# A two-block transformer kernel on one core: a mixer's first token tile transposed among the MLP's last row products, the second token tile transposed later at norm edges, and opening chunk pairs multiplied 512 columns wide outside the second block's mixers

## The chip, the cores and the metric

The kernel runs on 1 core of one Trainium2 chip. The metric is the device time of one execution in microseconds (us), and the median of several runs is compared. TensorE (PE) multiplies, VectorE (DVE) and ScalarE (ACT) do the elementwise work, GpSimd (POOL) computes small factors and starts some loads, SyncE (SP) starts the loads of weights.

## The reference, cut to what matters

A sequence of 256 tokens of width 1024 goes through two blocks, all in float32.

```python
def first_block(x, ...):                       # 2 layers
    for l in range(DEPTH):
        x = layer_norm(ALPHA * x + 0.5 * swiglu(x, wg0, wu0, wd0), ...)   # D_FF = 2816
        x = layer_norm(ALPHA * x + token_mix(x, w_in, w_out, ...), ...)   # three attention forms side by side
        x = layer_norm(ALPHA * x + 0.5 * swiglu(x, wg1, wu1, wd1), ...)
def second_block(x, ...):                      # 4 layers; mixers: delta rule, mLSTM, differential attention, delta rule
    for i in range(DEPTH_2):
        x = x + rms_norm(mixer_i(rms_norm(x, g0)), g1)
        x = x + rms_norm(square(relu(rms_norm(x, g2) @ w1)) @ w2, g3)     # D_FF_2 = 4096
```

## The kernel before

**Chunks.** All weights pass through the core once, as 365 chunks of 1 MB. A column chunk holds 256 output columns of a projection, with all 1024 input rows as 8 steps k of 128. A row chunk holds 256 input rows of a down projection with all 1024 output columns. Every chunk goes through SP's load into a slot of `raw` (5 slots), ACT's `split_high` (a rounded copy into one of 4 slots of `w_hi`, L461), DVE's `split_low` (the rest into `w_lo`, which lies over `raw`, L468), and three matmuls (hi by hi, hi by lo, lo by hi, `product`, L482 to L484). `load_chunk` waits until the chunk five places earlier has been used, `split_high` until the one four places earlier has. The semaphore `weights_used` counts used chunks. SP, ACT and DVE each go through the chunks in one fixed order, and each engine's queue is in order: a wait holds up all that is behind it.

**Stages.** First block: ffn(0,0), mix 0, ffn(0,1), ffn(1,0), mix 1, ffn(1,1). Second block, for i from 0 to 3: mixer i (delta rule, mLSTM, differential attention, delta rule) and mlp i. n0 is a stage's first chunk, and n0+1 and so on are the next. The MLP's order is hidden 0, hidden 1, hidden 2, rows 0, hidden 3, rows 1, hidden 4, rows 2, and so on to three row chunks at the end. So n0+3 is rows 0, n0+4 hidden 3, n0+5 rows 1 and n0+6 hidden 4.

**Between stages (an edge).** The sums y of a stage lie in PSUM banks 0 to 3, two banks for each tile of 128 tokens. `last_rows` (L624) finishes them bank by bank with the last row chunks. DVE and ACT then make the next input of tile 0 and of tile 1. PE transposes it in halves of four 128x128 blocks (`turn_bank`, L890 on: L897, or L895 as a matmul with a diagonal of token factors, which takes two passes), ACT copies the bank to aT_hi (L904), and DVE writes the rest to aT_lo (L910). A norm edge (in and after the first block) has x as input (written at L965). For the edges into ffn and mix, PE does a part of tile 0's transposes inside `last_rows` (`turn_first`). In the second block the input H is x times a gain; its token factor comes through POOL and a diagonal (L1743), but the third mixer takes H without the factor (`factor_behind`).

**The opening (`open_stage`, L566).** A stage's first two chunks n0 and n0+1 are column chunks that are multiplied in pieces, so that tile 0 can run while tile 1 is still being made: n0 steps 0 to 3, n0+1 steps 0 to 3, n0 steps 4 to 7, then `turn_tile(1)` (PE waits there for tile 1's input), n0+1 steps 4 to 7, and then tile 1 of both chunks. Before the MLPs after the delta rule ("early" edges) n0 has all of tile 0 first. All matmuls of the opening move 256 columns. n0 counts as used three quarters through the opening, n0+1 at its end; chunk n0 accumulates in bank 0, n0+1 in bank 1.

**The MLP's first hidden chunks.** Hidden 0 and 1 come out with tokens on the partitions, so PE transposes them (`turn_hidden`, L695): both in the middle of hidden 2, into banks 2 and 6. ACT copies (L700) and DVE writes the rest (L704). From hidden 2 on, the product stands the other way round (`wide_product`, L512 and L514) and needs no transposes. Hidden 3 writes banks 6 and 7.

Of the kernel before, what the change touches and what calls it, by code (L numbers as in the profile page):

```python
# [8 lines left out]
ALU = mybir.AluOpType  # L9
# [243 lines left out]
def two_block_model(nc, w, out):  # L253
# [311 lines left out]

    def open_stage(pe, n, edge):  # L566
# [8 lines left out]
        if n == 0:  # L575
            for q in range(4):
# [3 lines left out]
                tokens_steps(pe, 0, 0, 0, FIRST[0][q])  # L580
            turn_tile(pe, edge, 1)
            wait_part(pe, first_lo, lo_ready, 1, 0)
            tokens_part(pe, 1, 1, 0, 0)
            for half in range(2):
                turned_set(2 + half)
                last = tokens_part(pe, 0, 0, 1, half)
            last.then_inc(weights_used, 1)
            wait_part(pe, first_lo, lo_ready, 1, 1)
            tokens_part(pe, 1, 1, 0, 1)
            for half in range(2):  # L590
                last = tokens_part(pe, 1, 1, 1, half)
# [19 lines left out]
        tokens_part(pe, n, 0, 0, 1)  # L611
        turn_tile(pe, edge, 1)
        tokens_part(pe, n + 1, 1, 0, 1)
# [10 lines left out]
    def last_rows(pe, chunks, turn, turn_next=None):  # L624
# [3 lines left out]
        for b in range(4):  # L628
            t, c = b // 2, slice(b % 2 * 512, b % 2 * 512 + 512)
            for q, (n, l_hi, l_lo, wait) in enumerate(chunks):  # L630
# [5 lines left out]
                for r in range(2):  # L636
                    if b == 3 and turn_next is not None and (q, r) in turns:
# [68 lines left out]
    def hidden_made(dve, hid, s, gate, up, gates):  # L706
# [3 lines left out]
        nc.vector.tensor_tensor(hidden_buffer(s), gate, up, ALU.mult).then_inc(hid_made, 1)  # L710
# [35 lines left out]
    def ffn_scalar(act, l, j):  # L746
# [3 lines left out]
        for u, (kind, s) in enumerate(FFN_ORDER):  # L750
# [2774 lines left out]
```

## Time and profile before

| what | value |
| --- | --- |
| median of 3 runs | 2362.12 us (2359.69 to 2362.32) |
| the profiled execution's own time | 2360.35 us |
| its span, first to last instruction | 2358.6 us |
| granted TensorE clock, mean over the span | 0.999 of full speed |
| PE busy | 2325.4 us, 16820 matmuls |
| DVE, ACT, POOL busy | 1567.7, 1157.1 and 159.1 us |
| moved by DMA | 405.14 MB, mean 172 GB/s |

A row of the timeline gives the start, the time taken, the engine, the line, output<-inputs, shapes and count; in brackets stands the idle time just before and who ended it. The ends of matmuls are modelled, so that the time of one matmul in steady flow is read from the distance between two starts.

### The profile page before, as it was taken

Reading aid. Unit: us, or ns where it says so; the run is one execution under the profiler, and the core shown is the slowest. Engines: PE = TensorE matmul, PEld = TensorE weight load, DVE = VectorE, ACT = ScalarE, POOL = GpSimd, SP = SyncE. Lnnn points to the kernel's source line nnn. Section 1 sums busy time; section 2 is a strip of 40 time slices with the busy share of each in tenths; the row PEclk is TensorE's granted clock in tenths of the full one; section 3 lists DMA queues with packets and bytes.
Section 4 is the critical chain, followed back from the end, with each engine's and each line's share of the span. In section 5 each row is a group of like instructions: output and inputs, shape, how many; then the busy total and the mean of one; then the engine's idle time right before and its main releaser. Section 6 shows DMA issues by size and latency. Waiting matters only on the chain. (4 is left out here: it accounts for less than half of the span.)

```text
span 2358.6 us, 39266 instructions
## 1 busy us (share of the span) xinstructions
PE 2325.4 (99%) x16820; PEld 2062.5 (87%) x16820; DVE 1567.7 (66%) x2133; ACT 1157.1 (49%) x1573; POOL 159.1 (7%) x177
## 2 busy tenths in 40 slices
PE   9999999999999999999999999999999999999998
PEld 8889888888889888899888899888898888998887
DVE  5566775666576865768666657766677656867665
ACT  5444744435435644466554445534465334665432
POOL 0100000020000100002210000100001001012000
PEclk9999999999999999999999999999999999999999
DMA  7766355666655466453265644556445565433662
GB/s 247 244 214 137 108 186 189 214 187 214 209 148 150 127 210 208 145 168 109 73 214 189 205 154 143 181 194 213 154 142 177 187 206 156 139 110 108 205 210 94
DMA packets 320829, 405.14 MB, mean 172 GB/s; under 512 B 48720, under 2 KB 281264, under 8 KB 320656
## 3 DMA queue, kind: packets, MB, share of 16 engines
q1 hardware_dynamic: 314992, 383.50, 51.6%
q0 software_dynamic: 5664, 19.13, 2.6%
q8 instruction: 133, 2.18, 0.4%
q14 instruction: 40, 0.33, 0.0%
HBM read 401.55 MB, written 1.05 MB: 171 GB/s over the span
## 5 line engine op out<-in xcount | busy, mean ns | idle before, releaser
L468 DVE TENSOR_TENSOR w_lo<-raw,w_hi 128x2048 fp32r<-128x2048 f32 (+1 forms) x355 | 796.4, 2267 | 60.5 <-ACT w_hi L461 59.6
L461 ACT CAST w_hi<-raw 128x2048 fp32r<-128x2048 f32 (+1 forms) x355 | 672.1, 1894 | 303.4 <-PE ps L484 227.6
L512 PE MATMUL ps<-aT,w_hi 128*128 128x512 f32 x2048 | 511.3, 392 | 0.0
L512 PEld LDWEIGHTS ps<-aT,w_hi 128*128 128x128 f32 x2048 | 373.3, 188 | 70.2
L482 PE MATMUL ps<-w_hi,h_hi 128*128 128x512 f32 x864 | 339.2, 393 | 0.7 <-DVE h_lo L1970 0.6
L483 PE MATMUL ps<-w_lo,h_hi 128*128 128x512 f32 x864 | 337.4, 391 | 0.0
L484 PE MATMUL ps<-w_hi,h_lo 128*128 128x512 f32 x864 | 336.3, 389 | 0.0
L482 PE MATMUL ps<-w_hi,aT 128*128 128x256 f32 (+2 forms) x992 | 300.6, 303 | 6.8 <-DVE aT L910 4.6
L514 PEld LDWEIGHTS ps<-aT,w_lo 128*128 128x128 f32 x2048 | 279.4, 190 | 20.0
L484 PE MATMUL ps<-w_hi,aT 128*128 128x256 f32 (+2 forms) x992 | 294.0, 296 | 0.0
L483 PE MATMUL ps<-w_lo,aT 128*128 128x256 f32 (+2 forms) x992 | 294.0, 296 | 0.0
L514 PE MATMUL ps<-aT,w_lo 128*128 128x256 f32 x2048 | 285.6, 282 | 0.0
L482 PE MATMUL ps<-aT,w_hi 128*128 128x256 f32 (+1 forms) x792 | 230.2, 291 | 0.0
L483 PE MATMUL ps<-aT,w_hi 128*128 128x256 f32 (+1 forms) x792 | 223.8, 283 | 0.0
L484 PE MATMUL ps<-aT,w_lo 128*128 128x256 f32 (+1 forms) x792 | 223.7, 282 | 0.0
L482 PEld LDWEIGHTS ps<-w_hi,aT 128*128 128x128 f32 x992 | 189.4, 191 | 17.1 <-DVE aT L910 7.5
L484 PEld LDWEIGHTS ps<-w_hi,aT 128*128 128x128 f32 x992 | 189.4, 191 | 5.2
L483 PEld LDWEIGHTS ps<-w_lo,aT 128*128 128x128 f32 x992 | 189.6, 191 | 4.6
L484 PEld LDWEIGHTS ps<-w_hi,h_lo 128*128 128x128 f32 x864 | 162.2, 188 | 34.7
L482 PEld LDWEIGHTS ps<-w_hi,h_hi 128*128 128x128 f32 x864 | 162.6, 188 | 33.9 <-DVE h_lo L1970 2.0
L483 PEld LDWEIGHTS ps<-w_lo,h_hi 128*128 128x128 f32 x864 | 162.6, 188 | 29.7
L857 DVE TENSOR_TENSOR ws<-ws,ps 128x512 f32<-128x512 f32 x52 | 35.8, 688 | 183.3 <-ACT ws L838 183.3
(397 smaller groups left out, 2687.0 us busy)
## 6 DMA issues: line engine op xcount, KB each, us to landing
raw<-in_mlp_w SPq DMA_DIRECT2D x124, 1024.0 KB, 5.3
raw<-in_ffn_wg SPq DMA_DIRECT2D x43, 1024.0 KB, 5.3
raw<-in_ffn_wu SPq DMA_DIRECT2D x43, 1024.0 KB, 5.3
raw<-in_ffn_wd SPq DMA_DIRECT2D x40, 1024.0 KB, 4.9
raw<-in_gdn_w_in SPq DMA_DIRECT2D x32, 1024.0 KB, 5.9
raw<-in_mlstm_w_in SPq DMA_DIRECT2D x12, 1024.0 KB, 5.4
raw<-in_diff_w_in SPq DMA_DIRECT2D x12, 1024.0 KB, 5.2
raw<-in_w_in SPq DMA_DIRECT2D x8, 1024.0 KB, 5.2
```

The source lines that it names most:

```text
L461: nc.scalar.copy(used_part(hi_slot(n), n), used_part(raw_slot(n), n)).then_inc(hi_ready, 1)
L468: nc.vector.tensor_tensor(used_part(lo_slot(n), n), used_part(raw_slot(n), n), used_part(hi_slot(n), n).bitcast(F32), ALU.subtract).then_i ...
L482: nc.tensor.matmul(dst, l_hi, r_hi, start=start, stop=False)
L483: nc.tensor.matmul(dst, l_hi, r_lo, start=False, stop=False)
L484: return nc.tensor.matmul(dst, l_lo, r_hi, start=False, stop=stop)
L512: nc.tensor.matmul(ps[:, bank + ft, :], hi[:, k, c], aT[:, k, :], start=k == 0, stop=False)
L514: last = nc.tensor.matmul(ps[:, bank + ft, 0:SEQ], lo[:, k, c], aT_hi[:, k, :], start=False, stop=k == KT - 1)
L857: nc.vector.tensor_tensor(by_blocks(gate[2]), by_blocks(gate[2]), half_of(4 + 2 * (s % 2), 0), ALU.add).then_inc(gate_act, 1)
```

## The change

1. **Openings in pairs.** `open_paired` takes the place of `open_stage` in three ffn stages, both mix stages and all four MLPs (nine openings); ffn(0,0) and the four mixers of the second block keep `open_stage`. Of tile 0, steps 0 to 3 are as before, chunk by chunk. For the rest of tile 0 (on early edges for nothing of it) and for all of tile 1, one matmul moves 512 columns, 256 of n0 and 256 of n0+1. Where the slots of `w_hi` and `w_lo` wrap round differently, the hi by lo product stays 2 x 256; that is so in ffn(0,1), mix 1, mlp 1 and mlp 2. Tile 0 of both chunks is now in bank 0 and tile 1 in bank 1, and both chunks count as used at the opening's end. The readers (`pair_view`) wait for that.
2. **Second tile later.** On norm edges PE does 7 steps of tile 0 of both chunks before it turns to tile 1's transposes, instead of 6; at the mixers with a diagonal it does two more steps of n0+1.
3. **Mixer's tile 0 inside the last rows.** For mixers 1 to 3, `last_rows` of the MLP before contains one half (mixers 1, 3) or both halves (mixer 2) of tile 0's transposes. ACT's and DVE's part of them moves forward accordingly.
4. **Hidden 1 of the MLP** is transposed inside rows 0 (bank 7). PE waits for its `h_lo` between the two halves of hidden 3. On ACT and DVE its two instructions are behind the splits of n0+6.

```diff
+    def pair_steps(pe, n, t, steps):
+        swapped = slots_swapped(n)
+        both = ps[:, t, :].rearrange("p (a c) -> p a c", a=2)
+        for k in steps:
+            hi = of_both(w_hi, turn_of[n] % SPLIT, SPLIT, k)
+            x_hi, x_lo = (x_part[:, k, t * P:(t + 1) * P] for x_part in (aT_hi, aT_lo))
+            nc.tensor.matmul(both, x_hi, hi, start=k == 0, stop=False)
+            if swapped[0] == swapped[1]:
+                nc.tensor.matmul(both, x_hi, of_both(w_lo, lo_at[n], RAW, k), start=False, stop=False)
+            else:
+                for a in range(2):
+                    nc.tensor.matmul(ps[:, t, pair_half(n, a)], x_hi, by_cols(lo_slot(n + a))[:, k, :], start=False, stop=False)
+            last = nc.tensor.matmul(both, x_lo, hi, start=False, stop=k == KT - 1)
+        return last
+    def open_paired(pe, n, edge):
...
+        one_part(pe, n, 0, 0, first)
+        if edge["early"]:
+            turned_set(1)
+            one_part(pe, n, 0, 0, second)
+        pe.wait_ge(lo_ready, n + 2)
+        one_part(pe, n, 1, 0, first)
+        if edge["early"]:
+            turn_tile(pe, edge, 1)
+            one_part(pe, n, 1, 0, second)
+        else:
+            turned_set(1)
+            ahead = 7 if edge.get("late") else 6
+            pair_steps(pe, n, 0, range(4, ahead))
+            turn_tile(pe, edge, 1)
+            pair_steps(pe, n, 0, range(ahead, KT))
+        turned_set(2)
+        pair_steps(pe, n, 1, first)
+        turned_set(3)
+        pair_steps(pe, n, 1, second).then_inc(weights_used, 2)
@@ open_stage
+        ahead = 2 if edge.get("late") else 0
+        tokens_steps(pe, n + 1, 1, 0, range(4, 4 + ahead))
         turn_tile(pe, edge, 1)
-        tokens_part(pe, n + 1, 1, 0, 1)
+        tokens_steps(pe, n + 1, 1, 0, range(4 + ahead, KT))
@@ last_rows
+                    if b == 3 and mixer_next is not None and (q, r) in mixer_turns(mixer_next):
+                        turn_mixer(pe, mixer_next, mixer_turns(mixer_next).index((q, r)))
+    def mixer_turns(q):
+        return ((1, 0), (2, 0)) if factor_behind(q) else ((2, 1),)
@@ mlp_tensor
-        def turn_two():
-            turn_hidden(pe, hid0, 0, 2)
-            turn_hidden(pe, hid0 + 1, 1, 6)
+        inside = {2: lambda: turn_hidden(pe, hid0, 0, 2), 3: lambda: pe.wait_ge(hid_lo, hid0 + 2)}
+        open_paired(pe, n0, edge)
...
+                hidden_rows(pe, n0 + u, hid0 + s, s, (lambda: turn_hidden(pe, hid0 + 1, 1, 7)) if s == 0 else None)
-            if s == 3:
-                pe.wait_ge(hid_lo, hid0 + 2)
@@ mlp_vector
             for c in split_ahead(MLP_ORDER, u):
                 split_low(dve, n0 + c)
+            if (kind, s) == ("rows", 0):
+                turned_hidden_vector(dve, hid0 + 1, 1, 7)
+                hidden_split(dve, hid0 + 2, 2)
@@ addnorm_vector
             token_factors(dve, a + 1)
+            for half in range(len(mixer_turns(a + 1))):
+                turned_vector(dve, xpass, 0, half)
         weighted_y(1, 1)
-        if following:
-            turned_vector(dve, xpass, 0, 0)
         added(1)
```

On PE, before, at the end of mlp 0, the last two products of `last_rows` (h_hi and h_lo are the hidden activations), tile 0's transposes for the mLSTM mixer, and its first product:

```order
L482 MATMUL ps<-w_hi,h_hi 128x512
L483 MATMUL ps<-w_lo,h_hi 128x512
L484 MATMUL ps<-w_hi,h_lo 128x512
L482 MATMUL ps<-w_hi,h_hi 128x512
L483 MATMUL ps<-w_lo,h_hi 128x512
L484 MATMUL ps<-w_hi,h_lo 128x512
L895 MATMUL ps<-ws 128x128 x8
L482 MATMUL ps<-w_hi,aT 128x256
```

And now at the same place:

```order
L482 MATMUL ps<-w_hi,h_hi 128x512
L483 MATMUL ps<-w_lo,h_hi 128x512
L484 MATMUL ps<-w_hi,h_lo 128x512
L986 MATMUL ps<-ws 128x128 x4
L482 MATMUL ps<-w_hi,h_hi 128x512
L483 MATMUL ps<-w_lo,h_hi 128x512
L484 MATMUL ps<-w_hi,h_lo 128x512
L986 MATMUL ps<-ws 128x128 x4
L482 MATMUL ps<-w_hi,aT 128x256
```

The first half moved ahead of the last product; the second is behind it.

On ACT, before, in the MLP after the mLSTM mixer (mlp 1), from the first activation of the opening pair on (the casts L461 are the splits of n0+4, n0+5, n0+6 in turn; L838 is hidden 2's copy):

```order
L833 ACTIVATE ws<-ps 128x512 [waits weights_used]
L461 CAST w_hi<-raw 128x2048 [waits weights_used,raw_landed1]
L833 ACTIVATE ws<-ps 128x512 [waits weights_used]
L700 CAST h_hi<-ps 128x512 [waits hidden_turned] x2
L461 CAST w_hi<-raw 128x2048 [waits weights_used,raw_landed2]
L838 COPY ws<-ps 128x512 [waits hidden_made,weights_used]
L461 CAST w_hi<-raw 128x2048 [waits weights_used,raw_landed3]
```

And now:

```order
L912 ACTIVATE ws<-ps 128x512 [waits weights_used]
L461 CAST w_hi<-raw 128x2048 [waits weights_used,raw_landed1]
L912 ACTIVATE ws<-ps 128x512 [waits weights_used]
L782 CAST h_hi<-ps 128x512 [waits hidden_turned]
L461 CAST w_hi<-raw 128x2048 [waits weights_used,raw_landed2]
L917 COPY ws<-ps 128x512 [waits hidden_made,weights_used]
L461 CAST w_hi<-raw 128x2048 [waits weights_used,raw_landed3]
L782 CAST h_hi<-ps 128x512 [waits hidden_turned]
```

The copy of hidden 1 is now behind the casts of n0+5 and n0+6, and each of those waits for its chunk's landing.

On DVE now, at the same place, from the products of hidden 0 and 1 on (the first L468 is n0+4's, the two after L937 are n0+5's and n0+6's):

```order
L793 TENSOR_TENSOR ws<-ws 128x512 [waits gate_activated] x2
L786 TENSOR_TENSOR h_lo<-ps,h_hi 128x512 [waits hidden_hi_ready]
L468 TENSOR_TENSOR w_lo<-raw,w_hi 128x2048 [waits hi_ready]
L935 TENSOR_TENSOR ws<-ws,ps 128x512 [waits gate_activated,weights_used]
L937 SCALAR_TENSOR_TENSOR ws<-ws 128x512 [waits gate_activated]
L468 TENSOR_TENSOR w_lo<-raw,w_hi 128x2048 [waits hi_ready] x2
L786 TENSOR_TENSOR h_lo<-ps,h_hi 128x512 [waits hidden_hi_ready]
```

The second L786, for which PE waits inside hidden 3, stood right behind the first one before.

## Rows read from the trace of the kernel before

**Rows 1.** The page, part 1: busy time and share of the span.

```profile
PE 2325.4 (99%) x16820; PEld 2062.5 (87%) x16820; DVE 1567.7 (66%) x2133; ACT 1157.1 (49%) x1573; POOL 159.1 (7%) x177
```

**Rows 2.** PE's waits: total us, times, longest us.

```profile
PE ps L482 <- DVE aT L910: 4.6, 8, 1.4
PE ps L897 <- DVE x L965: 2.0, 5, 0.5
```

**Rows 3.** Timeline inside ffn(0,0), steady flow of 512 and 256 columns.

```profile
72.32 1.98 PE L512 MATMUL ps<-aT,w_hi 128*128 128x512 f32 x8
74.13 1.12 PE L514 MATMUL ps<-aT,w_lo 128*128 128x256 f32 x8
75.08 2.00 PE L512 MATMUL ps<-aT,w_hi 128*128 128x512 f32 x8
```

**Rows 4.** Timeline of a norm edge, ffn(0,1) to ffn(1,0).

```profile
506.69 0.28 PE L482 MATMUL ps<-w_hi,aT 128*128 128x256 f32 x1
...
510.70 1.42 DVE L965 SCALAR_TENSOR_TENSOR x<-ws,small,gb 128x512 f32<-128x512 f32 x2
...
511.51 1.32 PE L897 MATMUL ps<-consts,x 128*128 128x128 f32 x8 [0.35 <-DVE x L965]
...
512.20 1.25 ACT L904 CAST aT<-ps 128x512 fp32r<-128x512 f32 x2 [4.31 <-PE ps L897]
...
512.58 0.36 PE L482 MATMUL ps<-w_hi,aT 128*128 128x256 f32 x1
...
512.82 1.35 DVE L910 TENSOR_TENSOR aT<-ps,aT 128x512 fp32r<-128x512 f32 x2 [0.70 <-ACT aT L904]
```

**Rows 5.** Timeline of the edge from mlp 0 into the mLSTM mixer.

```profile
1375.48 0.29 DVE L1743 TENSOR_SCALAR ws<-consts,small 128x128 f32<-128x128 f32 x1 [1.24 <-POOL small L1769]
...
1376.71 1.95 PE L895 MATMUL ps<-ws 128*128 128x128 f32 x16
...
1379.16 0.39 PE L482 MATMUL ps<-w_hi,aT 128*128 128x256 f32 x1 [0.51 <-DVE aT L910]
...
1385.28 0.36 PE L482 MATMUL ps<-w_hi,aT 128*128 128x256 f32 x1
```

**Rows 6.** Timeline of the edge from mlp 1 into the differential attention.

```profile
1679.99 1.03 PE L897 MATMUL ps<-consts,ws 128*128 128x128 f32 x8
...
1682.39 0.39 PE L482 MATMUL ps<-w_hi,aT 128*128 128x256 f32 x1 [1.36 <-DVE aT L910]
```

**Rows 7.** Timeline of mlp 1 from its opening's end (1513.45).

```profile
1513.45 2.00 PE L512 MATMUL ps<-aT,w_hi 128*128 128x512 f32 x8
...
1516.24 1.03 PE L695 MATMUL ps<-consts,ws 128*128 128x128 f32 x8
...
1520.11 0.59 ACT L838 COPY ws<-ps 128x512 f32<-128x512 f32 x1 [0.34 <-PE ps L514]
...
1523.98 1.92 ACT L461 CAST w_hi<-raw 128x2048 fp32r<-128x2048 f32 x1 [3.28 <-DMA raw<-in_mlp_w]
...
1525.38 1.98 PE L512 MATMUL ps<-aT,w_hi 128*128 128x512 f32 x8
...
1525.93 2.29 DVE L468 TENSOR_TENSOR w_lo<-raw,w_hi 128x2048 fp32r<-128x2048 f32 x1 [0.23 <-ACT w_hi L461]
```

**Rows 8.** DMA issues at 1510.8 (n0+5), 1210.4, 1513.6, 1816.6, 2184.5 (n0+6), 122.8: us to landing.

```profile
raw<-in_mlp_w SPq DMA_DIRECT2D x1, 1024.0 KB, 4.8
...
raw<-in_mlp_w SPq DMA_DIRECT2D x1, 1024.0 KB, 10.2
...
raw<-in_mlp_w SPq DMA_DIRECT2D x1, 1024.0 KB, 10.3
...
raw<-in_mlp_w SPq DMA_DIRECT2D x1, 1024.0 KB, 8.5
...
raw<-in_mlp_w SPq DMA_DIRECT2D x1, 1024.0 KB, 6.7
...
ws<-in_ffn_wd SPq DMA_DIRECT2D x1, 1024.0 KB, 7.6
```

More of the change, by code:

```diff
@@ L564, in tokens_tile, with slots_swapped, pair_half, pair_view @@
             last.then_inc(weights_used, 1)
+    def slots_swapped(n):
+        return turn_of[n] % SPLIT == SPLIT - 1, lo_at[n] == RAW - 1
+    def pair_half(n, a):
+        half = 1 - a if slots_swapped(n)[0] else a
+        return slice(half * CW, (half + 1) * CW)
+    def pair_view(n, a):
+        return ps[:, 0:2, pair_half(n, a)]
+    def of_both(parts, at, n_slots, k):
+        first, step = (0, n_slots - 1) if at == n_slots - 1 else (at, 1)
+        return parts[:, first:first + step + 1:step, k * CW:(k + 1) * CW]
@@ new lines, in one_part @@
+    def one_part(pe, n, a, t, steps):
+        hi, lo = by_cols(hi_slot(n + a)), by_cols(lo_slot(n + a))
+        s = slice(t * P, (t + 1) * P)
+        for k in steps:
+            product(pe, ps[:, t, pair_half(n, a)], aT_hi[:, k, s], aT_lo[:, k, s], hi[:, k, :], lo[:, k, :],
+                    a == 0 and k == 0, a == 1 and k == KT - 1)
+    def open_paired(pe, n, edge):
+        xpass = edge["xpass"]
+        turned_set = lambda e: pe.wait_ge(aT_lo_set.sem, aT_lo_set.count(xpass, e))
+        first, second = range(0, 4), range(4, KT)
+        if not edge["early"]:
+            turn_tile(pe, edge, 0, edge.get("begun", 0))
+        turned_set(0)
+        pe.wait_ge(lo_ready, splits_made[n])
+        one_part(pe, n, 0, 0, first)
[17 more added lines that the diff above has]
+        pair_steps(pe, n, 1, second).then_inc(weights_used, 2)
@@ L848, in mlp_vector @@
                 if s == 1:
[L849 to L850 removed]
+                    turned_hidden_vector(dve, hid0, 0, 2)
             elif kind == "hidden" and s == MLP_STEPS - 1:
@@ L898, in turn_bank, with turned_scalar @@
         last.then_inc(turned.sem, 1)
-    def turned_scalar(act, xpass, t):
-        for half in range(2):
+    def turned_scalar(act, xpass, t, halves=(0, 1)):
+        for half in halves:
             act.wait_ge(turned.sem, turned.count(xpass, 2 * t + half))
@@ L1774, in addnorm_scalar @@
         early = a % 6 == 0
+        inside = range(len(mixer_turns(a + 1))) if into_mixer else ()
         for b in range(4):
@@ L1784, in addnorm_scalar @@
                 x_squares(act, a + 1, 0)
+                turned_scalar(act, xpass, 0, inside)
         if into_mixer:
-            turned_scalar(act, xpass, 0)
+            turned_scalar(act, xpass, 0, [half for half in range(2) if half not in inside])
             x_squares(act, a + 1, 1)
```

78 lines of the change are left out of this document (42 added, 36 removed).

## The prediction

> **What bounds the kernel now.** I read the page's first part: the reader is to see that PE is busy for 2325.4 us, 99% of the span, while DVE stands at 66% and ACT at 49% [rows 1]. So time comes out of this kernel only as fewer or cheaper PE cycles, or as one of PE's few waits gone, and it is lost wherever PE is made to wait. The second view is PE's list of waits: 4.6 us of opening products that wait for DVE's second half of a turned tile, and 2.0 us of transposes that wait for x, in five places [rows 2]. Third come the timelines: one steady stretch for the price of a matmul, three edges between stages, and an MLP from its opening's end. Last the DMA issues, because the change makes PE wait for work that stands behind two casts, and these stand behind landings.
>
> **Prices.** In steady flow eight matmuls of 512 columns take 1.81 us from start to start (74.13 less 72.32), 226 ns each, and eight of 256 columns 0.95 us, 119 ns each [rows 3]. Two of 256 merged into one of 512 give back 2 x 119 - 226 = 12 ns.
>
> **Gain a, tile 1 in pairs.** A step has three pairs of matmuls. All three merge in five stages, two in the four with swapped slots. Eight steps: 8 x 3 x 5 + 8 x 2 x 4 = 184 merged pairs, x 12 ns = 2.2 us. They are PE time itself, with nothing beside it to hide it.
>
> **Gain b, five norm edges.** Before, PE did 36 products of tile 0 (4.3 us) and came to tile 1's transposes too early for x: it began them at 511.51 after 0.35 us of idleness, and tile 0 of n0+1 went on at 512.58 [rows 4]. The four steps left are 12 x 0.119 = 1.43 us, so tile 1's products began at 514.0. Now 24 single products and three paired steps (9 x 0.226) stand ahead: 2.86 + 2.03 = 4.89 us after 506.69, which is 511.6, when the first half of x is there. ACT's copies, 0.69 us behind the first transpose (512.20 less 511.51), and DVE's, 0.62 behind them (512.82 less 512.20), are as late as before less the bit that x allows: the first half of aT_lo is written at 512.82 + 0.68 = 513.5 before, and 513.6 to 513.7 now, since PE turns 0.1 us later. PE has only one paired step (0.68 us) left after the turns, until 513.3. So the x wait becomes a shorter wait at L482 for L910, 0.36 us, and tile 1 starts at 513.66 instead of 514.0: 0.35 gained. The five waits for x sum to 2.0 us [rows 2], one is 0.35 here, so I take 0.4 each: 2.0 us.
>
> **Gain c.** Mlp 1 and mlp 2 have tile 0's second four steps in pairs, 4 x 2 x 12 ns = 0.1 us each: 0.2 us. (In the five norm edges this is inside b; the early edges have none.)
>
> **Gain d, three mixer edges.** At the mLSTM the diagonal is there at 1375.48 + 0.29 = 1375.77, before the 16 transposes at 1376.71, and PE then waits 0.51 us [rows 5]. One half (eight two-pass blocks, 0.98 us) now goes ahead of the last product of 3 x 0.226 = 0.68 us, so ACT and DVE have that and the second half as cover: the wait goes, and with it 0.1 us of the turns' ends; I give back 0.1 for tile 1's diagonal. 0.5 to 0.6 us, and as much at the second delta rule: 1.1 us. At the differential attention both halves go ahead, and a wait of 1.36 us goes [rows 6]; but tile 1 of the input is made no earlier, and two steps more of n0+1 cover only part of it, so I give back about 0.5: 0.9 us. Together 2.0 us.
>
> **Gains: 2.2 + 2.0 + 0.2 + 2.0 = 6.4 us.**
>
> **The loss: a new wait in each MLP.** Hidden 1's copy on ACT and split on DVE now stand behind the splits of n0+5 and n0+6, and PE asks for them in the middle of hidden 3. PE comes there 11.93 + 12 x 0.23 = 14.7 us after the opening's end E (1525.38 less 1513.45) [rows 7]. Before, the cast of n0+6 already waited 3.28 us for its landing and began at 1523.98, 10.5 us after E [rows 7]. Behind this landing come cast 1.92, split 2.29 and hidden 1's half 0.68 [rows 4, 7], with handovers 5.0 us: ready at E + 15.5 against 14.7. So even if nothing lands later, mlp 1 waits 0.8 us, and mlp 0 0.7 (its load, 10.2 us [rows 8]). In mlp 2 and mlp 3 (8.5 and 6.7 us [rows 8]) it would be ready at 13.7 and 11.9, in time.
>
> But n0 now counts as used only at the opening's end, where it did three quarters through. SP issued n0+5 at 1510.8 and n0+6 at 1513.6 [rows 8]; now both go at E + 0.2. Alone n0+5 landed in 4.8 us; a 1 MB load 0.41 us behind another took 7.6, so 1 MB ahead costs 2.8 us [rows 8]. Two things follow. First, n0+5 lands at about E + 6.4 (0.2 + 4.8 + half of the 2.8), and its own chain is then cast 1.92, about 0.8 for hidden 2's copy (0.59) and its handover, 1.4 of DVE's work on hidden 2 (two 128x512 instructions at L965's price), 2.29, 2.29 and 0.68: 9.4 us, ready at E + 15.8, a wait of 1.1 us [rows 4, 7, 8]. Second, n0+6 has 1 MB more in front: between nothing (the loads share what the engines have left) and 2.8. I take the middle, 1.4, because n0+6 already shares with POOL's gain loads, and n0+5 had most of its 4.8 us done when it was issued before. Waits: 2.1, 2.2, 1.1, 1.1 = 6.5 us. Bounds: 1.5 (nothing later, n0+5's chain in time) and 3.5 + 3.6 + 1.8 + 1.1 = 10.0.
>
> The Trainium skill (*DMA: Bandwidth & Descriptors*, section "Issuing engines are not separate DMA queues") says that loads started by different engines run on the same 16 DMA engines and interleave. By that rule the extra megabyte would be paid in full, and the sum would be 10.0 - 6.4 = +3.6 us. The trace leans that way: n0+6 took 10.3 us beside POOL's loads and n0+5 4.8 us ahead of them [rows 8].
>
> **What costs nothing.** Holding n0 and n0+1 until the opening's end makes hidden 0's activation later by a quarter of an opening, but hidden 0 is turned only in the middle of hidden 2, 2.8 us after E, and its activation, gate product and handovers take some 1.6; if the cover were gone it would be a wait of up to 0.5 us per MLP. The second bank of an opening is read at its end as before.
>
> **Sum.** -6.4 + 6.5 = +0.1 us. The profiled execution's own time, 2360.35 us, is 1.8 us below the median 2362.12; I apply the difference to the median: 2362.2 us. With the bounds of the load: -4.9 (2357.2) to +3.6 (2365.7). What a measurement can tell from no change is about 0.2%, 4.7 us.
>
> **Rivals.**
> 1. *The gains stand and the wait is small* (0.28). PE's 14.7 us may be covered: if n0+6 lands no later than before, the net is 1.5 - 6.4 = -4.9, 2357.2 us; if it lands earlier, since n0+5 no longer takes its place among POOL's loads, no wait is left and it is 2355.7. For it: n0+5 and n0+6 were 2.8 us apart before and most of the slowness is then POOL's. Against it: the 3.28 us that the cast waited [rows 7].
> 2. *Slower: the loads pile up* (0.22). One mechanism: POOL's loads and now n0+5 stand in front of n0+6. POOL's cost it 10.3 - 4.8 = 5.5 us in mlp 1, 5.4, 3.7 and 1.9 in the others [rows 8]. If n0+5 costs as much again, the four waits are 6.1, 6.3, 2.7 and 1.1 = 16.2 us, net +9.8: 2371.9 us. It decides once the waits sum to over 6.4 + 4.7 = 11.1 us, which is n0+6 landing 2.8 us later than before on average, just beyond my bound.
> 3. *The pairs don't flow* (inside "same", 0.05). One matmul that reads two slots, with two pieces of 256 in its moving operand, is in no row of before. Below, nothing excludes 226 ns; above, at 238 ns the merge gives nothing, and gains a and c (2.4 us) fall out: 2364.6 us. The Trainium skill (*TensorE: Matmul & The Clock Gate*, section "Back-to-back issue gap") puts a gap of a few ns on each matmul whatever its width, so that two of 256 would cost about one gap more than one of 512, an estimate of 2.5 ns in place of 12; the sum would be about 1.9 us higher. The trace disagrees: 119 ns twice is 12 more than 226 [rows 3].
>
> **How the numbers follow.** Forecast, no measurable change: 0.50 (its own range 2357.4 to 2366.8). Faster by over 0.2%, rival 1's outer part: 0.28. Slower by over 0.2%, rival 2: 0.22. A range that leaves out a tenth on each side goes from 2356 (rival 1 with no wait) to 2368 (between my upper bound and rival 2).
>
> **What the changed profile would show.** Steps a and c: starts of paired matmuls 226 ns apart. Step b: the five waits of transposes for x gone or under 0.1 us, and in their place waits of some 0.3 us for the second part of tile 1. Step d: the opening product of the three mixers waits under 0.2 us, where one waited 1.36. The loss: in all four MLPs PE waits in the middle of hidden 3 for DVE's h_lo, 1 to 2 us; n0+5 and n0+6 issued together at the opening's end, n0+6 landing some 11.5 us later in mlp 0 and 1. The prediction is wrong if these two landings are far from 6.4 and 11.9, or if the wait at hidden 3 ends on something else than the cast of n0+6: then the order of ACT's and DVE's queues matters less than I say.

## The result and the profile after

The changed kernel takes 2376.02 us (median of 4 runs, 2373.68 to 2380.38), the kernel before 2361.11 us (median of its 4 runs in the same comparison, 2359.69 to 2362.32). The ratio is 1.0066, 95% interval 1.0048 to 1.0083: 14.9 us slower. The prediction said 2362.2 us, range 2356 to 2368, with a chance of 0.22 for slower.

The page of the changed kernel, part 1, and PE's list of waits (total us, times, longest us). They answer to [rows 1] and [rows 2].

```profile
PE 2330.1 (98%) x16568; PEld 2053.1 (86%) x16568; DVE 1568.6 (66%) x2133; ACT 1156.3 (49%) x1573; POOL 158.4 (7%) x177
```

```profile
PE ps L512 <- DVE h_lo L786: 10.7, 4, 3.4
...
PE ps L482 <- DVE aT L1001: 2.3, 5, 0.5
...
PE ps L596 <- DVE aT L1001: 0.2, 1, 0.2
```

There are 252 matmuls fewer, and yet PE is busy for 4.7 us longer: fewer matmuls can't do that, so some ran slower. The wait for x is gone from the list, and the wait for aT_lo fell from 4.6 to 2.3 us. A new line leads it: four waits, one in each MLP, 10.7 us in all. The timeline of mlp 0 from ACT's cast of n0+5 on shows what the wait is made of (the opening ends at 1209.06; it answers to [rows 7], which is mlp 1).

```profile
1217.41 1.91 ACT L461 CAST w_hi<-raw 128x2048 fp32r<-128x2048 f32 x1 [4.37 <-DMA raw<-in_mlp_w]
...
1219.22 0.57 ACT L917 COPY ws<-ps 128x512 f32<-128x512 f32 x1
...
1219.90 0.69 DVE L935 TENSOR_TENSOR ws<-ws,ps 128x512 f32<-128x512 f32 x1 [3.94 <-ACT ws L917]
...
1220.55 1.92 ACT L461 CAST w_hi<-raw 128x2048 fp32r<-128x2048 f32 x1 [0.75 <-DMA raw<-in_mlp_w]
...
1221.23 4.48 DVE L468 TENSOR_TENSOR w_lo<-raw,w_hi 128x2048 fp32r<-128x2048 f32 x2
1222.37 0.58 ACT L782 CAST h_hi<-ps 128x512 fp32r<-128x512 f32 x1
...
1225.64 0.68 DVE L786 TENSOR_TENSOR h_lo<-ps,h_hi 128x512 fp32r<-128x512 f32 x1
```

Read it backwards. h_lo ends at 1226.32. Ahead of it DVE has no gap back to 1219.90: two instructions of hidden 2 and two splits. It could not start sooner because ACT's copy L917 stood behind the cast of n0+5, and that cast waited 4.37 us for its landing. h_hi, by contrast, was there at 1222.95. So in mlp 0 the wait hangs on the landing of n0+5, not on n0+6 and not on ACT's copy of hidden 1. PE at the same place:

```profile
1220.99 2.00 PE L512 MATMUL ps<-aT,w_hi 128*128 128x512 f32 x8
1222.83 1.11 PE L514 MATMUL ps<-aT,w_lo 128*128 128x256 f32 x8
1226.37 3.00 PE L512 MATMUL ps<-aT,w_hi 128*128 128x512 f32 x8 [2.43 <-DVE h_lo L786]
1229.16 1.82 PE L514 MATMUL ps<-aT,w_lo 128*128 128x256 f32 x8
1230.83 0.39 PE L482 MATMUL ps<-w_hi,h_hi 128*128 128x512 f32 x1
```

The wait is only the first half of the damage. Eight matmuls of 512 columns take 1.84 us before the wait (1220.99 to 1222.83) and 2.79 us after it. The windows of PE there (us, PE busy with count, granted clock, DMA share, GB/s):

```profile
1217.00:1223.00 6.00, 6.00 (x31) 1.00 0.99 342
1223.00:1226.00 3.00, 0.94 (x8) 1.00 0.91 306
1226.00:1228.00 2.00, 1.63 (x6) 0.83 0.03 9
1228.00:1231.00 3.00, 3.00 (x13) 0.54 0.00 0
1231.00:1233.00 2.00, 2.00 (x10) 1.00 0.42 49
```

After the pause the granted clock goes from full level (2.4 GHz) to half of it (1.2 GHz) for some 3 us. The half of hidden 3 behind the wait takes 4.46 us (1226.37 to 1230.83), where the same half took 2.79 us in the kernel before. In mlp 1, 2 and 3 it takes 4.3, 4.3 and 4.2 us, and there the half clock reaches a little into the next product.

The landings, worked out from issue and landing of each SP load, in us from the opening's end (n0+5 was issued 2.7 us ahead of it before and 0.2 us behind it now, n0+6 at 0.2 before and 0.6 now):

| MLP | n0+5, before | n0+5, now | n0+6, before | n0+6, now | h_lo of hidden 1 ends, now | PE comes for it |
| --- | --- | --- | --- | --- | --- | --- |
| 0 | 2.1 | 8.3 | 10.4 | 11.5 | 17.3 | 14.7 |
| 1 | 2.1 | 8.4 | 10.5 | 11.4 | 17.4 | 14.7 |
| 2 | 2.0 | 9.3 | 8.7 | 12.6 | 18.2 | 14.7 |
| 3 | 2.1 | 8.3 | 6.9 | 11.2 | 17.2 | 14.7 |

The norm edge of [rows 4], now, PE alone:

```profile
511.51 1.19 PE L988 MATMUL ps<-consts,x 128*128 128x128 f32 x8
512.46 0.48 PE L596 MATMUL ps<-w_hi,aT 128*128 128x512 f32 x1
...
513.51 0.50 PE L596 MATMUL ps<-w_hi,aT 128*128 128x512 f32 x1
```

No wait for x, the pair step behind the turn at 512.46, and tile 1 at 513.51 where before it was 514.0.

### The profile page after: what moved, and what is told of

It is laid out like the page before. It is cut to its first block and busy times, and to the rows that moved or that the text cites. A ratio compares the mean times of both kernels' runs of the same rounds, so it can differ in the third digit from the quotient of the medians.

```text
span 2373.6 us, 38758 instructions
## 1 busy us (share of the span) xinstructions
PE 2330.1 (98%) x16568; PEld 2053.1 (86%) x16568; DVE 1568.6 (66%) x2133; ACT 1156.3 (49%) x1573; POOL 158.4 (7%) x177
## 3 DMA queue, kind: packets, MB, share of 16 engines
q8 instruction: 131, 2.15, 0.4%
## 5 line engine op out<-in xcount | busy, mean ns | idle before, releaser
L468 DVE TENSOR_TENSOR w_lo<-raw,w_hi 128x2048 fp32r<-128x2048 f32 (+1 forms) x355 | 796.9, 2269 | 68.9 <-ACT w_hi L461 68.1
L461 ACT CAST w_hi<-raw 128x2048 fp32r<-128x2048 f32 (+1 forms) x355 | 672.0, 1893 | 325.8 <-PE ps L484 229.9
L512 PE MATMUL ps<-aT,w_hi 128*128 128x512 f32 x2048 | 514.7, 393 | 10.8 <-DVE h_lo L786 10.7
L512 PEld LDWEIGHTS ps<-aT,w_hi 128*128 128x128 f32 x2048 | 374.7, 189 | 83.0 <-DVE h_lo L786 11.5
L482 PE MATMUL ps<-w_hi,aT 128*128 128x256 f32 (+2 forms) x792 | 243.8, 308 | 5.2 <-DVE w_lo L450 2.6
L484 PE MATMUL ps<-w_hi,aT 128*128 128x256 f32 (+2 forms) x792 | 237.5, 300 | 0.0
L483 PE MATMUL ps<-w_lo,aT 128*128 128x256 f32 (+2 forms) x792 | 237.4, 300 | 0.0
L482 PEld LDWEIGHTS ps<-w_hi,aT 128*128 128x128 f32 x792 | 150.9, 191 | 15.5 <-DVE aT L1001 5.3
L484 PEld LDWEIGHTS ps<-w_hi,aT 128*128 128x128 f32 x792 | 151.0, 191 | 5.2
L483 PEld LDWEIGHTS ps<-w_lo,aT 128*128 128x128 f32 x792 | 151.1, 191 | 4.7
```

The source lines that it names most:

```text
L461: nc.scalar.copy(used_part(hi_slot(n), n), used_part(raw_slot(n), n)).then_inc(hi_ready, 1)
L468: nc.vector.tensor_tensor(used_part(lo_slot(n), n), used_part(raw_slot(n), n), used_part(hi_slot(n), n).bitcast(F32), ALU.subtract).then_i ...
L482: nc.tensor.matmul(dst, l_hi, r_hi, start=start, stop=False)
L483: nc.tensor.matmul(dst, l_hi, r_lo, start=False, stop=False)
L484: return nc.tensor.matmul(dst, l_lo, r_hi, start=False, stop=stop)
L512: nc.tensor.matmul(ps[:, bank + ft, :], hi[:, k, c], aT[:, k, :], start=k == 0, stop=False)
```

## The experiments

The start of each stage's opening in the trace, less the start in the kernel before, tells where time goes. It is worked out from the first opening product of each stage.

| us later than before | mix 0 | mLSTM | differential attention | second delta rule | end of span |
| --- | --- | --- | --- | --- | --- |
| changed kernel | +1.1 | +2.5 | +5.3 | +10.4 | +15.0 |
| e1_order | +0.1 | -3.4 | -4.9 | -5.1 | -0.2 |
| e8_order_no_mixer_turns | +2.2 | -0.3 | -0.6 | -0.8 | +4.6 |

(The first column has only ffn(0,0) behind it, whose opening is unchanged. The kernel's start differs between the profiled executions, most in e6, e7 and e8, as is told at e7.)

### e1_order: hidden 1 ahead of the splits

```diff
@@ mlp_scalar
+            if (kind, s) == ("rows", 0):
+                turned_hidden_scalar(act, hid0 + 1, turned_before["mlp", i] + 2, 1, 7)
             for c in split_ahead(MLP_ORDER, u):
                 split_high(act, n0 + c)
-            if (kind, s) == ("rows", 0):
-                turned_hidden_scalar(act, hid0 + 1, turned_before["mlp", i] + 2, 1, 7)
@@ mlp_vector
                 if s > 2:
                     hidden_split(dve, hid0 + s, s)
+                else:
+                    turned_hidden_vector(dve, hid0 + 1, 1, 7)
             for c in split_ahead(MLP_ORDER, u):
                 split_low(dve, n0 + c)
             if (kind, s) == ("rows", 0):
-                turned_hidden_vector(dve, hid0 + 1, 1, 7)
                 hidden_split(dve, hid0 + 2, 2)
```

> The changed kernel, with hidden 1's copy ahead of the cast of n0+6 on ACT and its h_lo ahead of the splits of n0+5 and n0+6 on DVE. Theory A (the loss is the order of these two instructions behind late landings, 11.3 us of waits in the middle of hidden 3, and the granted clock that falls to half behind each wait, some 1.7 us each): h_lo is there about 2 us before PE asks, all four waits and all four clock drops go, 18 us less than the changed kernel: about 2358 us. Theory B (the loss is the late issue of n0+5 and n0+6 behind the paired opening, whatever the order): PE then waits as long for the split of n0+5 at rows 1 instead, and the time stays at 2372 to 2376.

Measured: 2358.41 us (median of 11), before 2361.36 beside it, ratio 0.9985 (0.9976 to 0.9994). Theory A, to half a microsecond. DVE at mlp 0 (its opening ends at 1207.39):

```profile
1218.69 0.69 DVE L937 SCALAR_TENSOR_TENSOR ws<-ws 128x512 f32<-128x512 f32 x1
1219.30 0.68 DVE L786 TENSOR_TENSOR h_lo<-ps,h_hi 128x512 fp32r<-128x512 f32 x1
1219.90 4.48 DVE L468 TENSOR_TENSOR w_lo<-raw,w_hi 128x2048 fp32r<-128x2048 f32 x2
```

h_lo ends 12.6 us after the opening's end instead of 17.3. The landings have not moved (n0+5 8.1, n0+6 11.2 us after the opening's end): the late landings alone cost nothing, and theory B is out. The order of two small instructions, one on ACT and one on DVE, is worth 17.6 us.

### e2_turn_as_before: part 4 undone

```diff
-        inside = {2: lambda: turn_hidden(pe, hid0, 0, 2), 3: lambda: pe.wait_ge(hid_lo, hid0 + 2)}
+        def turn_two():
+            turn_hidden(pe, hid0, 0, 2)
+            turn_hidden(pe, hid0 + 1, 1, 6)
```

(with the waits, banks and the order of ACT and DVE as before.)

> The changed kernel with its fourth part undone: hidden 1 is transposed in the middle of hidden 2 into bank 6, as before, with ACT's and DVE's order of before; parts 1, 2 and 3 stay. Theory A: no wait at hidden 3, so about 2358 us, as e1_order within 1 us (the place of the transposes costs nothing, only the order behind the splits does). Theory B: 2372 to 2376.

Measured: 2362.37 us, before 2361.36, ratio 0.9998 (0.9990 to 1.0007). The loss is gone, but it is 4 us above e1_order where I expected 1. Its list of waits has a line that e1_order's lacks:

```profile
PE ps L777 <- DVE ws L793: 2.6, 5, 0.6
```

With n0 and n0+1 used only at the opening's end, hidden 1's activation is too late for a transpose in the middle of hidden 2: about 0.5 us in each of four MLPs (the fifth of these waits is in ffn(0,0)). That is 2 of the 4 us; the rest isn't accounted for, and the two profiled executions differ by 0.6 us only. So the pairs need part 4, and what was wrong with it is the place of its instructions behind the splits. The prediction's part on what costs nothing looked at hidden 0's activation alone.

### e3_mlp_unpaired: the MLP's openings chunk by chunk

```diff
@@ mlp_tensor
-        open_paired(pe, n0, edge)
+        open_stage(pe, n0, edge)
@@ mlp_scalar
-                nc.scalar.activation(by_blocks(gate[s]), pair_view(n0, s), ACT.Relu).then_inc(gate_act, 1)
+                nc.scalar.activation(gate[s], ps[:, s, :], ACT.Relu).then_inc(gate_act, 1)
```

> The changed kernel with the four MLP openings chunk by chunk as before (n0 released three quarters through), part 4 kept. Theory A: n0+5 is issued 2.8 us earlier and lands about 2 us after the opening's end instead of 8.3, so h_lo waits for n0+6 alone (landing 10.4, 10.5, 8.7, 6.9 after the opening's end, plus 5.0, against 14.7): waits of 0.7, 0.8, 0 and 0 us, no clock drop; the pairs' 1.2 us are lost: 2376 - 18 + 1.5 + 1.2 = 2360.7 us. Theory B: likewise about 2359, but e1_order and e2_turn_as_before stay slow. If the extra time sat in the order alone and not in the landing, the waits would stay near 2.6 us each and the time at 2376.

Measured: 2359.85 us, before 2361.36, ratio 0.9994 (0.9985 to 1.0003). n0+5 lands 2.1 to 2.2 us after the opening's end again, n0+6 at 8.8, 8.9, 8.9 and 7.2, and h_lo ends at 13.7, 13.7, 13.7 and 13.3, ahead of PE's 14.7: no wait at all, where I had 0.7 and 0.8. (Part of that is n0+6's landing at 8.8 and 8.9 instead of the 10.4 and 10.5 that I had.) Both halves are needed for the loss: the order that hangs hidden 1 behind the splits, and the pairing that holds n0's slot and makes n0+5 late. Either cure takes it away.

### e4_filled_wait and e5_fill_ten: the clock

```diff
+        def filled():
+            pe.wait_ge(hid_made, hid0 + 3)
+            keep_busy(pe, 20, bank=4)
+            pe.wait_ge(hid_lo, hid0 + 2)
```

> The changed kernel with 20 extra 128x128 matmuls on the identity (109 ns each, 2.2 us) in front of PE's wait in the middle of hidden 3, into bank 4, which is free there; nothing they write is read. Theory A: the wait ends at the same time, the fill lies inside it, but PE isn't idle for over 1.3 us any more, so that the clock stays at full level and about 1.7 us are saved in each MLP: 2376 - 6.7 = 2369.3 us. Rival C (the clock falls for another reason, such as the paired matmuls' load): the drops stay and the time is 2376 us or more.

Measured: 2377.13 us, before 2361.36, ratio 1.0063 (1.0050 to 1.0075): no gain. But the fill was too long: its 20 matmuls ran as 40 passes, 4.39 us, and PE went on at 1227.53.

```profile
1222.19 1.12 PE L514 MATMUL ps<-aT,w_lo 128*128 128x256 f32 x8
1223.14 4.63 PE L955 MATMUL ps<-consts 128*128 128x128 f32 x40
1227.53 2.09 PE L512 MATMUL ps<-aT,w_hi 128*128 128x512 f32 x8
1229.46 1.11 PE L514 MATMUL ps<-aT,w_lo 128*128 128x256 f32 x8
```

The half behind it takes 2.88 us (1227.53 to 1230.41), not 4.46: what the clock gave back, the fill took. Hence the same with 10:

```diff
-            keep_busy(pe, 20, bank=4)
+            keep_busy(pe, 10, bank=4)
```

> e4_filled_wait with 10 extra matmuls instead of 20. In e4's trace each of them ran as two passes, so that the 20 took 4.4 us (4.39 from 1223.14 to 1227.53) and outran the wait by 1.2 us; the second half of hidden 3 then ran at full clock. Ten take 2.2 us and fit into the waits. Theory A (idleness before it is what takes the clock down): drops gone, waits as in the changed kernel, 4 x 1.7 = 6.7 us less than the changed kernel: about 2369.5 us. Rival C (e4 ran at full clock only because its fill was longer than the wait): the drops come back, 2376 us.

Measured: 2369.27 us, before 2361.77, ratio 1.0035 (1.0022 to 1.0049), 6.75 us less than the changed kernel. PE and the windows:

```profile
1222.84 2.40 PE L955 MATMUL ps<-consts 128*128 128x128 f32 x20
1225.48 2.11 PE L512 MATMUL ps<-aT,w_hi 128*128 128x512 f32 x8 [0.25 <-DVE h_lo L786]
```

```profile
1223.00:1226.00 3.00, 2.75 (x22) 1.00 0.67 235
1226.00:1228.00 2.00, 2.00 (x12) 1.00 0.00 0
1228.00:1231.00 3.00, 3.00 (x17) 1.00 0.39 97
```

The halves behind the waits take 2.9 us in all four MLPs in place of 4.2 to 4.5, and the granted clock stays at full level. So the drop is a consequence of PE's idleness before it. In the changed kernel's trace it costs 1.67 us in mlp 0 (4.46 less 2.79), an estimate of 6.7 us for four. The agreement of that with the 6.75 us is in part luck, because the waits did not stay the same: h_lo came 0.3, 1.2 and 1.2 us earlier in mlp 1, 2 and 3 than in the changed kernel's trace. In the profiled executions the difference is 7.7 us, 1.8 of it from halves that begin earlier.

### e6_dve_order_only: one split less ahead of h_lo

```diff
@@ mlp_vector
+            if (kind, s) == ("rows", 0):
+                turned_hidden_vector(dve, hid0 + 1, 1, 7)
             for c in split_ahead(MLP_ORDER, u):
                 split_low(dve, n0 + c)
             if (kind, s) == ("rows", 0):
-                turned_hidden_vector(dve, hid0 + 1, 1, 7)
                 hidden_split(dve, hid0 + 2, 2)
```

> The changed kernel with one instruction moved: DVE's h_lo of hidden 1 ahead of the split of n0+6 (still behind n0+5's); ACT's copy stays behind the cast of n0+6. Theory A, chain of n0+5: DVE is busy without a gap from hidden 2's two instructions to h_lo, and one split of 2.2 us less in front brings h_lo from 2.4 to 3.5 us late to 0.2 to 1.3 us late; no clock drop where the wait is under 1 us: 18 us of loss becomes 2 to 4, so 2360 to 2362 us. The prediction's chain of n0+6 (its cast ends near the opening's end plus 13.4) gives h_lo no later than 14.1 against PE's 14.7 and adds nothing. Rival (ACT's order carries the loss): 2370 us or more.

Measured: 2361.55 us, before 2361.77, ratio 0.9997 (0.9988 to 1.0006). Two waits are left, in mlp 1 and 2, and behind the longer one the clock holds (eight matmuls of 512 columns in 1.95 us, granted 1.00):

```profile
PE ps L512 <- DVE h_lo L786: 1.9, 2, 1.3
```

```profile
1831.90 2.11 PE L512 MATMUL ps<-aT,w_hi 128*128 128x512 f32 x8 [1.32 <-DVE h_lo L786]
1833.85 1.12 PE L514 MATMUL ps<-aT,w_lo 128*128 128x256 f32 x8
```

Moving one DVE instruction over one split gives 14.5 of e1_order's 17.6 us, with ACT's order untouched.

### e7_order_not_late and e8_order_no_mixer_turns: what parts 2 and 3 are worth

```diff
@@ e7, in open_paired and open_stage
-            ahead = 7 if edge.get("late") else 6
+            ahead = 6
-        ahead = 2 if edge.get("late") else 0
+        ahead = 0
@@ e8
-        hidden_last_rows(pe, MLP_ORDER, n0, hid0, 3 * DEPTH + 2 * i + 1, mixer_next=2 * i + 2 if i + 1 < DEPTH_2 else None)
+        hidden_last_rows(pe, MLP_ORDER, n0, hid0, 3 * DEPTH + 2 * i + 1)
```

(Both are e1_order with this edit. In e8 also `begun=0` and ACT's and DVE's part of tile 0 at its old place.)

> e1_order with part 2 of the change undone: 6 steps of tile 0 ahead of tile 1's transposes at norm edges, none at the mixers. By the prediction's step b the five norm edges give back 0.35 to 0.4 us each; the pairs alone (36 products become 24 + 6 x 0.227) bring PE to tile 1's transposes 0.2 us earlier still, so the x waits are 0.5 to 0.7 us. With 0.1 to 0.2 at two mixers: 2.0 us more than e1_order, 2360.4. Rival (DVE's aT_lo bounds tile 1, whatever the order): same as e1_order within 0.5 us.

> e1_order with part 3 undone: tile 0's transposes of mixers 1 to 3 all behind the MLP's last product, ACT's and DVE's part of them at its old place. By step d of the prediction 2.0 us more than e1_order. By the traces of the changed kernel the three openings start 0.6, 1.4 and 0.6 us earlier but lose 0.3, 0.7 and 0.3 of it again before tile 1: then 1.3 us more, 2359.7 us.

Measured: e7 2362.51 us, before 2361.77, ratio 1.0002 (0.9993 to 1.0011); e8 2360.90 us, ratio 0.9994 (0.9985 to 1.0003). Against e1_order's 2358.41 these are 4.1 and 2.5 us, more than expected, but the executions differ in two things that have nothing to do with the edit. One is the pauses told of below. The other is at the kernel's start: in the profiled executions of e6, e7 and e8 PE waits 2.0 to 2.2 us for a split of the first chunks and then runs at half clock for some 3 us, where in e1_order's it waits 1.5 us and the clock holds. The wait and the window behind it, in e7:

```profile
14.13 0.39 PE L482 MATMUL ps<-w_hi,aT 128*128 128x256 f32 x1 [2.03 <-DVE w_lo L450]
```

```profile
14.80:18.20 3.40, 3.40 (x19) 0.54 1.09 362
```

Single stages can be compared without either. In e7 the x waits are back:

```profile
PE ps L989 <- DVE x L1057: 2.2, 5, 0.5
```

The five openings at norm edges are 0.35, 0.20, 0.35, 0.23 and 0.35 us shorter than before in e7, and 0.65, 0.62, 0.65, 0.52 and 0.69 us in e1_order: the pairs give 1.5 us there and the later turn 1.65. At the mLSTM and at the second delta rule, where part 2 was expected to give 0.1 to 0.2 us, the opening of e7 ends 0.67 and 0.63 us later than e1_order's, counted from the opening's end of the MLP before: part 2 is worth 1.65 + 1.3 = 2.95 us. In e8 the wait for aT_lo is back at 4.6 us in 8 places with its longest at 1.4, as in [rows 2]; counted in the same way, the openings of the three mixers end 0.47, 0.76 and 0.47 us later than e1_order's: part 3 is worth 1.7 us.

### e9_order_late_diff: the later turn at the third mixer too

```diff
-                    late=q and not factor_behind(q), fill=...
+                    late=bool(q), fill=...
```

> e1_order with part 2 at the third mixer too: two steps of n0+1 ahead of tile 1's transposes in the differential attention. In the changed kernel's trace PE waits 0.31 us there for tile 1's input; ACT's copies behind it bound tile 1's start (0.5 us of waiting for ACT later), so the gain is 0 to 0.3 us: 2358.2 us, the same as e1_order by measurement. The sum stops: no wait of over 0.5 us is left that this order table reaches.

Measured: 2358.41 us, before 2362.39, ratio 0.9986 (0.9977 to 0.9995); the same as e1_order. The differential attention's opening loses 0.7 us of its earlier start in both: nothing gained.

### e10_before_padded, e11_order_pad16, e12_order_pad32: pauses that no wait explains

Nearly all traces have pauses of PE in the two delta rules, among runs of 64x64 matmuls, that the profile calls issue. Their sums, from the distances between two starts (what they exceed the median for that instruction by, where it is over 0.25 us):

| kernel | first delta rule, us | second, us |
| --- | --- | --- |
| before | 2.6 | 0.9 |
| changed | 3.4 | 2.1 |
| e1_order | 2.9 | 4.8 |
| e2, e3, e4 | 3.5, 3.4, 3.6 | 2.5, 4.3, 2.4 |
| e5, e6, e7, e8, e9 | 2.6, 3.7, 3.6, 2.8, 3.0 | 2.6, 2.1, 3.1, 4.2, 2.4 |
| e10_before_padded | 0.6 | 0.7 |
| e11_order_pad16 | 1.1 | 0.8 |
| e12_order_pad32 | 0.0 | 3.2 |

In e1_order one of them is 4.52 us long, in the middle of a projection, and the clock drops behind it as it does behind a wait (256 columns in 0.21 to 0.22 us instead of 0.12):

```profile
2059.42 2.40 PE L2831 MATMUL ps<-ws 64*64 64x64 f32 x128 [0.27 <-DVE ws L3304]
2061.76 0.39 PE L482 MATMUL ps<-aT,w_hi 128*128 128x256 f32 x1
2066.66 0.37 PE L483 MATMUL ps<-aT,w_hi 128*128 128x256 f32 x1 [4.52 <-issue]
2066.83 0.41 PE L484 MATMUL ps<-aT,w_lo 128*128 128x256 f32 x1
2067.04 0.42 PE L482 MATMUL ps<-aT,w_hi 128*128 128x256 f32 x1
```

The trace shows what this pause waits for. A DMA queue of its own carries packets of 16,384 bytes of the kind "instruction", 131 in e1_order, 2.15 MB. None moves between 2061.8 and 2064.2, one moves from 2064.25 to 2065.27 (the DMA view of 2064.2 to 2065.3 has it alone), and PE goes on at 2066.66:

```profile
q8 instruction: 131, 2.15, 0.4%
...
q8 instruction: 1, 0.02, 5.8%
```

It is so every time: all 66 pauses that the table sums, in 14 traces, end 1.2 to 1.6 us after the end of such a packet. So they are waits for instructions, although a fetch alone, every few microseconds, doesn't always cause one.

The pad puts 32 or 16 short matmuls at the very start and changes nothing else (e10 is the kernel before, e11 and e12 are e1_order):

```diff
             keep_busy(pe, 4)
+            for _ in range(32):
+                nc.tensor.matmul(ps[:, 7, 0:1], ident, ident[:, 0:1], start=True, stop=True)
```

> The kernel before with 32 one-column float32 matmuls on the identity (64 passes, 128 instructions of PE with their weight loads, 2 to 3.5 us) at the very start, where PE waits 1.1 us for the first weights. They compute nothing that is read. Theory F (PE's instructions arrive in blocks, and where the delta rules' short matmuls outrun them depends on the position in the stream: the pauses that the trace calls issue are 2.6 and 0.9 us in the two delta rules of before, and 3.4 to 3.6 and 2.1 to 4.8 us in the changed kernels): the pause in the second delta rule grows to 2 us or more, and the time by 1 to 4 us beyond the pad's own cost of up to 2.4 us: 2363 to 2367 us. Rival G (the longer pauses come from the change itself, its loads or its order): 2.6 and 0.9 us stay, 2361 to 2363.5 us.

> e1_order with 16 such matmuls at the start (64 instructions). Theory F: the pauses in the delta rules change from 2.6 and 4.8 us, by up to 4 us in their sum either way, at unchanged work; with before's sum of 3.5 us it would be 2358.4 + 0.5 - 4 = 2355 us. Rival G: 2.6 and 4.8 us stay, 2359 us.

> e1_order with 32 such matmuls at the start (128 instructions). Theory F: another sum of pauses again, different from e1_order's and from e11_order_pad16's by over 0.5 us. Rival G: the same pauses in all three; the time 2358.4 plus up to 2.4 us.

Measured beside 2362.39 us of before: e10 2366.23 us, ratio 1.0022 (1.0012 to 1.0031); e11 2356.74 us, ratio 0.9976 (0.9967 to 0.9986); e12 2364.67 us, ratio 1.0010 (1.0001 to 1.0019). The pad of 32 was far dearer than I wrote: its 64 passes took 11.5 us in e10 and 9.3 in e12, and the first opening product starts 9.8 and 7.1 us later than in the kernel before, 1.3 us later with 16. In e10:

```profile
6.55 11.69 PE L576 MATMUL ps<-consts 128*128 128x1 f32 x64
18.09 0.56 PE L482 MATMUL ps<-w_hi,aT 128*128 128x256 f32 x1
```

The pauses moved at unchanged work. In the first delta rule this is clear of the spread: 0.6, 1.1 and 0.0 us with a pad, 2.6 to 3.7 us in the eleven traces without one. That is theory F, and rival G is out there. Its direction failed for e10, where the pauses shrank from 3.5 to 1.3 us in place of growing; e10's time lies in theory F's range by luck, because the pad cost 9.8 us and not 2.4. In the second delta rule it isn't shown: e10 keeps before's 0.9 us nearly (0.7), the traces without a pad already range from 0.9 to 4.8 us, and each kernel has one profiled execution, so that its spread from one execution to the next is not known. e11 does e1_order's work and some 1.3 us of padding, and its profiled span is 2352.5 us where e1_order's is 2358.3: the pauses fell from 7.7 to 1.9 us. PE's lines called issue in the list of waits of e1_order, and then of e11:

```profile
PE ps L483 <- issue: 4.5, 1, 4.5
...
PE ps L2831 <- issue: 2.0, 3, 1.2
```

```profile
PE ps L484 <- issue: 0.6, 1, 0.6
...
PE ps L483 <- issue: 0.2, 1, 0.2
...
PE ps L2833 <- issue: 0.2, 1, 0.2
```

e11_order_pad16 is 0.24% faster than the kernel before and 19 us faster than the changed one. Against e1_order the gain is open: the medians differ by 1.7 us only, the intervals of the two ratios overlap, and the profiled execution is one of e11's fastest and one of e1_order's slower ones.

## Why the prediction was wrong

**Gains a and c (pairs) were right.** The openings of the early MLPs are 0.31 us shorter and those with swapped slots 0.23, against 0.29 and 0.2 to 0.3 in the sum. The matmul over two slots of `w_hi` flows at 227 ns; rival 3 is out.

**Gain b (norm edges) was right.** With the pairs it is 0.66, 0.57, 0.64, 0.51 and 0.71 us, 3.1 in all, where the sum had 3.2 (2.0 and five stages' share of a, 1.2). One of the five, ffn(1,0), loses 0.4 us again later in the stage, at a late w_lo.

**Gain d (mixer edges) was a little too large:** 1.7 us against e8, 1.5 against the kernel before, for 2.0. Its parts were sized wrongly, since without the later turn (e7) the two mixers with a diagonal lose all of it. The third mixer starts 1.4 us earlier and gives back 0.7, not 0.5.

**The loss was in the right place and of the right kind, and its size was wrong: 17.4 to 18 us for 6.5.** The prediction's waits (2.1, 2.2, 1.1, 1.1 us) came out as 10.7 us of idleness in all (11.4 by the start of the half behind), with mlp 2 the worst, where it expected the least, as in mlp 3. The step that failed is "n0+5 lands at about E + 6.4", from 4.8 us alone and half of 2.8 for the load beside it. It landed at 8.3 to 9.3. n0+6 was right for mlp 0 and 1 (11.4 to 11.5 against 11.9), but for mlp 2 and 3, where I had added 1.4 to landings of 8.7 and 6.9, it came 4.0 and 4.3 us later than before. The 4.8 us for n0+5 were the wrong row: they were measured on a load issued 2.7 us ahead of the opening's end, before POOL's loads of 0.5 MB each, the first issued 0.2 to 0.5 us ahead of it and the second, which mlp 3 lacks, 0.1 to 0.4 us behind it. A single load issued 0.2 us behind the opening's end, where n0+5 now is, was also in [rows 8], as n0+6 of before: it took 10.2, 10.3, 8.5 and 6.7 us. n0+5 now takes 8.1, 8.2, 9.1 and 8.1. So in mlp 0, 1 and 2 a load issued at that moment was about as late without another of SP's behind it; in mlp 3, with one load of POOL's, it comes 1.4 us later than the single load did. The pair in ffn(0,0) whose second is the 7.6 us of [rows 8] took 5.5 and 7.6 us, and the single load just before it 5.4: there the first of two was hardly touched. The chain behind n0+5 was sized well: 8.9 us (1217.41 to 1226.32) for 9.4. With 8.3 in place of 6.4 the step gives 8.3 + 8.9 - 14.7 = 2.5 us, which is what mlp 0 shows. The range's upper bound took the wrong load: it varied n0+6 by 2.8 and left n0+5 as it was. The last sign of being wrong came true in its first half and not in its second: the wait ended on the chain of n0+5 and not on the cast of n0+6, and yet the order of the two queues decided everything (e1).

**The second cause was missing from the sum altogether.** Each wait cost some 1.7 us more in matmuls at half clock, 6.7 us by the estimate at e5. The kernel before had no row with a price for this: its longest pause of PE behind the first microseconds was 1.4 us, and the granted clock did not drop before PE's last matmul had ended. The price of idleness on PE was taken as its length.

**Rival 2** (loads pile up, 2371.9 us) was nearest, with the wrong load in it. The Trainium skill (*DMA: Bandwidth & Descriptors*, section "Issuing engines are not separate DMA queues") would have it that the loads of SP and POOL interleave, and the trace agrees: POOL's 0.5 MB load, issued within 0.2 us of n0+5, landed 8.6, 7.8 and 9.7 us after the opening's end in mlp 0, 1 and 2, where n0+5 landed at 8.3, 8.4 and 9.3.

**What is left over.** In the profiled executions the span grew by 15.0 us. 10.7 of waits and 6.7 of clock are 17.4; pauses in the delta rules add 2.0, the start of the kernel 1.1; less 6.4 of predicted gains that makes 14.1. e1_order has no loss in the MLPs, and its stages before the second delta rule stand at -5.1 us, in line with 5 to 6 us of gains.

**Open.** Why n0+6 lands earlier in e3 (8.9 us) than in before (10.4), with the same issue times, was not tried. The pauses in the delta rules are waits for instructions, but what makes a packet start late, and so fixes their length, was not settled: where they fall is not predicted, and e10 fell on the other side of its expectation. The Trainium skill (*Runtime: NRT & Kernel Launch*, section "Instruction fetch mechanics") says that instructions come in blocks of 16 KiB, which is 256 instructions, fetched while others run, at a cost that is mostly hidden. The trace agrees on the blocks: at 256 instructions each, the changed kernel's 131 packets of 16,384 bytes hold an estimated 33,536, and it has 33,136 matmuls and weight loads. It doesn't agree that they are hidden, with 1.3 to 7.7 us of pauses in the delta rules.

## What to carry to other kernels

When a semaphore makes a load start later, follow its landing to the end, and price it by a row of a load that was issued at the new moment, beside what other queues move then, not by its own row from the old moment; then look for the small instruction that stands behind them on an in-order engine. A change that delays a buffer and a change that queues work behind it can each be free alone (e1, e3) and cost 18 us together. A wait of TensorE costs its length, and where it was 2.4 to 3.4 us here, another 1.7 us at half clock behind it. Matmuls whose results nobody reads give that back as long as they are shorter than the wait.

## What the runs showed of the hardware that was not expected

- PE at full clock paused 2.4 to 3.4 us and then ran at half clock for some 3 us (0.54 to 0.83 granted). The same followed a pause of 4.5 us that no semaphore caused, and one of 2.0 us at the start of e7. In all 14 traces no pause of up to 1.75 us had a drop behind it, and two longer ones had none either: 1.9 us in the changed kernel and 2.45 us in e2, both in the second delta rule.
- PE's pauses called issue in the delta rules ranged from 1.3 to 7.7 us in sum over the profiled executions, and each ended 1.2 to 1.6 us after a packet of 16,384 bytes of instructions had moved. 64 instructions more at the start of the program (16 float32 matmuls with their weight loads, two passes each) went with 1.1 us of them in place of 2.9 in the first delta rule, a thousand microseconds later.
- One-column float32 matmuls are dear: a pass takes 112 ns from start to start at full clock, as much as the 128-column passes that filled the wait in e4. PE issued 64 of them without a pause, and still the granted clock fell to half, from 8.7 us on in e10 and from 10.7 us on in e12; a pass then took 213 ns, and the 256-column matmuls behind them 0.21 us. The 32 passes of e11 ran at full clock.
